# Moving the merge-gate jobs of a two-branch decoder block into nine dense head chunks, with a merged rotation and a shorter softmax

## The reference, cut to what matters

```python
def hybrid_mixer(h, w_in, ..., w_proj_a, w_proj_b, w_out, layer_idx):
    z = jnp.einsum('bsd,dn->bsn', h, w_in)
    qa, ka, va, ga, qb, kb, vb, gb, fl, ma, mb = jnp.split(z, idx, axis=-1)
    # 8 differential heads: partial rotation of q and k, two softmax maps, a = p0 - lam * p1
    oa = rmsnorm(diff_attention(rope(qa), rope(ka), va, lam), g_subln) * (1.0 - lam_init)
    ya = (oa * silu(ga)) @ w_proj_a
    # 8 forgetting ("fox") heads: one softmax map, bias from the summed log forget gates
    yb = (forgetting_attention(qb, kb, vb, log_f) * silu(gb)) @ w_proj_b
    m = jax.nn.sigmoid(ma) * ya + jax.nn.sigmoid(mb) * yb
    return jnp.einsum('bsd,de->bse', m, w_out)

def reference(x, ...):
    x = x + hybrid_mixer(rmsnorm(x, g_norm), ...)
    return rmsnorm(x, g_final)
```

## Time and profile before

| | us |
|---|---|
| median of 3 runs | 741.78 (741.42 to 742.18) |
| the profiled execution | 742.65 |
| its span, first to last instruction | 740.8 |
| TensorE busy | 729.5 (98%) |
| VectorE busy | 566.1 (76%) |
| ScalarE busy | 437.8 (59%) |
| GpSimd busy | 126.3 (17%) |

### The profile page before, as it was taken

How to read it: one execution, slowest core, us unless ns; L and a number is a source line. 1 busy time by engine, 2 the same in 40 slices (tenths; PEclk the granted TensorE clock), 3 DMA queues, 4 the chain that set the end, 5 groups by cost and what they waited for, 6 DMA issues and landing times.

```text
span 740.8 us, 9801 instructions
## 1 busy us (share of the span) xinstructions
PE 729.5 (98%) x3538; PEld 609.9 (82%) x3538; DVE 566.1 (76%) x746; ACT 437.8 (59%) x654; POOL 126.3 (17%) x153
## 2 busy tenths in 40 slices
PE   9999999999999999999999999999999999999996
PEld 6998888888888888888878888788888888888885
DVE  6775798788779878868979976979998757655552
ACT  7963767566656565665656766667567444444531
POOL 0000223103010203030615030704050000001110
PEclk9999999999999999999999999999999999999999
DMA  8668365776947686775576876666777756755632
GB/s 330 213 214 328 139 227 209 248 225 239 343 158 252 214 263 211 275 289 185 220 243 198 269 252 252 223 233 215 215 257 230 220 185 227 297 188 190 192 140 114
DMA packets 47230, 168.97 MB, mean 228 GB/s; under 512 B 5256, under 2 KB 5264, under 8 KB 46672
## 3 DMA queue, kind: packets, MB, share of 16 engines
q1 hardware_dynamic: 46064, 164.97, 65.1%
q10 hardware_dynamic: 864, 1.84, 0.7%
q0 software_dynamic: 256, 1.54, 0.5%
HBM read 166.23 MB, written 2.11 MB: 227 GB/s over the span
## 4 chain that ended last, share of the span: by engine, by line
PE 90%; POOL 4%; DVE 2%; issue 2%; DMA 1%; ACT 1%; SPq 0%; DVEq 0%; POOLq 0%; ACTq 0%
PE Z L338 27%; PE Z L340 27%; PE Z L339 27%; PE Z L499 3%; POOL rope_t L1223 3%; PE A L440 1%; DVE w_lo L841 1%; PE A L406 1%; DMA w_raw<-in_w_main 1%; PE B L422 1%; PE B L419 1%; POOL z_sb L1228 1%; PE Dk L431 1%; DVE gates L908 1%; POOL z_sb L1229 1%
## 5 line engine op out<-in xcount | busy, mean ns | idle before, releaser
L841 DVE TENSOR_TENSOR w_lo<-w_raw,w_hi 128x1024 fp32r<-128x1024 f32 (+1 forms) x240 | 290.4, 1215 | 111.3 <-ACT w_hi L610 108.7
L610 ACT ACTIVATE w_hi<-w_raw 128x1024 fp32r<-128x1024 f32 (+1 forms) x235 | 243.6, 1044 | 187.0 <-PE Z L340 164.5
L338 PE MATMUL Z<-w_hi,hT_hi 128*128 128x512 f32 (+2 forms) x720 | 274.6, 381 | 0.5 <-DVE w_lo L841 0.5
L340 PE MATMUL Z<-w_hi,hT_lo 128*128 128x512 f32 (+2 forms) x720 | 272.8, 379 | 0.0
L339 PE MATMUL Z<-w_lo,hT_hi 128*128 128x512 f32 (+2 forms) x720 | 272.6, 379 | 0.0
L338 PEld LDWEIGHTS Z<-w_hi,hT_hi 128*128 128x128 f32 x720 | 135.3, 188 | 26.6 <-issue 0.6
L340 PEld LDWEIGHTS Z<-w_hi,hT_lo 128*128 128x128 f32 x720 | 135.3, 188 | 25.7
L339 PEld LDWEIGHTS Z<-w_lo,hT_hi 128*128 128x128 f32 x720 | 135.4, 188 | 24.6
L338 PE MATMUL Z<-w_hi,sum_hi 128*128 128x512 f32 x256 | 101.2, 395 | 0.0
L340 PE MATMUL Z<-w_hi,sum_lo 128*128 128x512 f32 x256 | 99.9, 390 | 0.0
L339 PE MATMUL Z<-w_lo,sum_hi 128*128 128x512 f32 x256 | 99.7, 389 | 0.0
(11 more groups left out here) (184 smaller groups left out, 593.7 us busy)
## 6 DMA issues: line engine op xcount, KB each, us to landing
w_raw<-in_w_main SPq DMA_DIRECT2D x283, 512.0 KB, 4.2
x_and_g<-in_w_main SPq DMA_DIRECT2D x16, 512.0 KB, 6.3
w_raw<-in_w_fl SPq DMA_DIRECT2D x8, 264.0 KB, 3.1
o_T<-in_x SPq DMA_DIRECT2D x1, 2048.0 KB, 8.0
x_and_g<-in_xT SPq DMA_DIRECT2D x4, 256.0 KB, 5.9
gates<-c_rows_dram POOLq DMA_DIRECT2D x1, 1024.0 KB, 5.7
z_sb<-in_g_final SPq DMA_DIRECT2D x1, 1024.0 KB, 10.0
x_and_g<-in_xT ACTq DMA_DIRECT2D x3, 256.0 KB, 7.2
```

The costliest lines, as they stand in the source:

```text
L338: pe.matmul(acc, a_hi, b_hi, start=first, stop=False)
L340: return pe.matmul(acc, a_lo, b_hi, start=False, stop=last)
L610: act.activation(w_hi[:, t % RING, 0:cols_of(t)], weights(t), ACT.Copy).then_inc(hi_ready, 1)
L841: dve.tensor_tensor(w_lo[:, t % RING, 0:n], weights(t), w_hi[:, t % RING, 0:n].bitcast(fp32), ALU.subtract).then_inc(lo_ready, 1)
```

## The change

Chunks 3 to 11 carry twelve merge jobs each, chunk 12 carries four, and chunks 2, 13, 14, 15 and the fox projections carry none (`SUMS_IN`, `ORDER`). The number of jobs, their weights and their matmuls stay the same, and so does each group's order of forms. A chunk without merge jobs, and each projection, takes the other pair of PSUM banks than the one before it (`PAIR`), and `banks_free` waits for the last user of that pair. The places of the bursts X and Y are set for each kind of chunk. The rotation works on both token halves at once: four products and two sums of 128 x 64. The masked maximum gives the negative scaled value at once, so that the small multiplication behind it is gone. The two maps are combined in one pass, with the first normalizer carried to the output's scaling, where one small product is added. The last quarter row is squared on VectorE instead of ScalarE.

```diff
 FL_JOB, VG_JOB, PLAIN_JOB, MIXED_JOB = 8, 16, 20, 28
-FOX_JOB = MIXED_JOB + 16 * (N_HEADS - 3)
-FOX2_JOB = FOX_JOB + 16
-DIFF_JOB = FOX2_JOB + 8
+SUMS_IN = {3: 12, 4: 12, 5: 12, 6: 12, 7: 12, 8: 12, 9: 12, 10: 12, 11: 12, 2: 0, 12: 4, 13: 0, 14: 0, 15: 0}
+ORDER = {0: 'hhhhhhhh', 4: 'hshshshshhhh', 12: 'hshsshshsshshsshhsss'}
+CHUNK_JOB = [0, 0, PLAIN_JOB]
+for c in range(3, N_HEADS + 1):
+    CHUNK_JOB.append(CHUNK_JOB[-1] + len(ORDER[SUMS_IN[c - 1]]))
+FOX_JOB = CHUNK_JOB[N_HEADS]
+DIFF_JOB = FOX_JOB + 16
 OUT_JOB = DIFF_JOB + 16
 JOBS = OUT_JOB + 32
-HEAD_STEPS, SUM_STEPS = (0, 2, 4, 6, 8, 10, 12, 13), (1, 3, 5, 7, 9, 11, 14, 15)
-FOX_STEPS, FOX_SUM_STEPS = (0, 2, 4, 5, 8, 11, 14, 15), (1, 3, 6, 7, 9, 10, 12, 13)
-SUM_JOB = ([MIXED_JOB + 16 * c + u for c in range(N_HEADS - 3) for u in SUM_STEPS] + [FOX_JOB + u for u in FOX_SUM_STEPS])
+SUM_JOB = [CHUNK_JOB[c] + u for c in range(2, N_HEADS) for u, kind in enumerate(ORDER[SUMS_IN[c]]) if kind == "s"]
 SUM_OF = {job: s for s, job in enumerate(SUM_JOB)}
-X_AT = {21: 0, 28: 1, 38: 2, **{MIXED_JOB + 16 * (b - 2) + 4: b for b in range(3, N_HEADS)},
-        FOX2_JOB + 1: N_HEADS, DIFF_JOB + 1: N_HEADS + 1}
-Y_AT = {25: 0, 33: 1, 43: 2, **{MIXED_JOB + 16 * (b - 2) + 9: b for b in range(3, N_HEADS)}, FOX2_JOB + 5: N_HEADS}
+BURST_X, BURST_Y = {0: 2, 4: 4, 12: 5}, {0: 6, 4: 9, 12: 11}
+X_AT = {21: 0, 28: 1, 40: 2, **{CHUNK_JOB[b + 1] + BURST_X[SUMS_IN[b + 1]]: b for b in range(3, N_HEADS - 1)},
+        FOX_JOB + 2: N_HEADS - 1, FOX_JOB + 9: N_HEADS, DIFF_JOB + 1: N_HEADS + 1}
+Y_AT = {25: 0, 34: 1, 46: 2, **{CHUNK_JOB[b + 1] + BURST_Y[SUMS_IN[b + 1]]: b for b in range(3, N_HEADS - 1)},
+        FOX_JOB + 5: N_HEADS - 1, FOX_JOB + 13: N_HEADS}
 C_ZERO, C_MASK, C_TRI, C_IDENT, C_ONE = 0, P, 2 * P, 3 * P, 4 * P
...
+def max_count(heads):
+    return 2 * heads + 2 * max(0, heads - HEADS)
+
+
 def head_job(c, j):
     if c == 0:
         return j
-    return PLAIN_JOB + j if c == 2 else MIXED_JOB + 16 * (c - 3) + HEAD_STEPS[j]
+    return CHUNK_JOB[c] + [u for u, kind in enumerate(ORDER[SUMS_IN[c]]) if kind == "h"][j]
 def fox_job(n, j):
-    return FOX_JOB + FOX_STEPS[4 * n + j] if n < 2 else FOX2_JOB + 4 * (n - 2) + j
+    return FOX_JOB + 4 * n + j
...
 PARTS_AT = {PLAIN_JOB + 7: 0, MIXED_JOB + 2: 1, MIXED_JOB + 11: 2, MIXED_JOB + 18: 3}
-O_SPLIT_AT = {FOX_JOB - 20: 0, FOX_JOB - 14: 1, FOX2_JOB + 3: 2, FOX2_JOB + 4: 3}
+O_SPLIT_AT = {CHUNK_JOB[13] + 4: 0, CHUNK_JOB[13] + 7: 1, CHUNK_JOB[15] + 4: 2, FOX_JOB + 7: 3}
 HEAD_OF = {head_job(c, j): (c, j) for c in range(2, N_HEADS) for j in range(TILES)}
 FOX_OF = {fox_job(n, j): (n, j) for n in range(4) for j in range(4)}
 DIFF_OF = {diff_job(n, j): (n, j) for n in range(4) for j in range(4)}
+
+
+PAIR = [0, 1, 0, 1]
+for c in range(3, N_HEADS):
+    PAIR.append(0 if SUMS_IN[c] else 1 - PAIR[-1])
+for n in range(11):
+    PAIR.append(1 - PAIR[-1])
+LAST_PAIR = 1 - PAIR[-1]
+FIRST_SUM_FILL, FOX_FILL, DIFF_FILL, OUT_FILL = 4, 17, 21, 25
...
                 mm.then_inc(w_used, 1)
-            def banks_free(fill):
-
-                pe.wait_ge(evac[0], fill - 1)
-                pe.wait_ge(evac[1], fill - 1)
+            def banks_free(fill, pair):
+
+                before = [n for n in range(fill) if PAIR[n] == pair]
+                if before:
+                    pe.wait_ge(evac[0], before[-1] + 1)
+                    pe.wait_ge(evac[1], before[-1] + 1)
+                if pair == 1 and fill > FIRST_SUM_FILL:
+                    form_taken(FORMS * GROUPS - 2)
+                    form_taken(FORMS * GROUPS - 1)
             def z_tile(c, j):
-                tile(head_job(c, j), 1 if c == 2 else 0, hT_hi, hT_lo, 2 * j, 2, CHUNK, j == 0, j == TILES - 1)
+                tile(head_job(c, j), PAIR[fill_of(c)], hT_hi, hT_lo, 2 * j, 2, CHUNK, j == 0, j == TILES - 1)
...
                     if j == 0:
-                        banks_free(4 if c == 3 else fill_of(c) + 1)
+                        banks_free(fill_of(c), PAIR[fill_of(c)])
                     z_tile(c, j)
...
                 if j == 0:
-                    banks_free((18, 19, 19, 20)[n])
-                    if n == 2:
-                        form_taken(FORMS * GROUPS - 2)
-                        form_taken(FORMS * GROUPS - 1)
+                    banks_free(FOX_FILL + n, PAIR[FOX_FILL + n])
                 if n == 0:
                     pe.wait_ge(o_split, j // 2 + 1)
-                tile(fox_job(n, j), 1 if n == 2 else 0, oT_hi, oT_lo, 2 * j, 2, CHUNK, j == 0, j == 3)
+                tile(fox_job(n, j), PAIR[FOX_FILL + n], oT_hi, oT_lo, 2 * j, 2, CHUNK, j == 0, j == 3)
             for job in range(FOX_JOB, DIFF_JOB):
-                if job in FOX_OF:
-                    fox_tile(*FOX_OF[job])
-                else:
-                    sum_tile(SUM_OF[job])
+                fox_tile(*FOX_OF[job])
                 attention(job)
...
             def exps(h):
-                act.wait_ge(max_ready, h + 1)
-                maps, scale = (1, HD ** -0.5) if h < HEADS else (2, QK ** -0.5)
+                act.wait_ge(max_ready, max_count(h + 1))
+                maps, scale = 1 if h < HEADS else 2, -1.0
                 for i in range(maps):
...
                 for m in range(M_TILES):
-                    ins = act.activation(og[:, m, :], A[:, m * P:(m + 1) * P], ACT.Square,
+                    ins = act.activation(og[:, m, :], A[:, m * P:(m + 1) * P], ACT.Square, scale=inv[:, m:m + 1],
                                          accum_out=o_ssq[:, m:m + 1])
...
                     S = (B, C)[i]
-                    counted(dve.tensor_tensor_reduce(probs[:, i, 0:P], S[:, 0:P], add0, 1.0, NEG, ALU.add, ALU.max,
-                                                     row_max[:, 2 * i:2 * i + 1]))
-                    n = counted(dve.tensor_tensor_reduce(probs[:, i, P:3 * P], S[:, P:3 * P], add1, 1.0, NEG, ALU.add, ALU.max,
-                                                         row_max[:, 2 * i + 1:2 * i + 2]))
-                dve.wait_ge(dve_step, n)
-                if h < HEADS:
-                    ins = dve.tensor_scalar(neg_max[:, 0:2], row_max[:, 0:2], -(HD ** -0.5), None, ALU.mult)
-                else:
-                    ins = dve.tensor_scalar(neg_max[:], row_max[:], -(QK ** -0.5), None, ALU.mult)
-                ins.then_inc(max_ready, 1)
+                    scale = -(HD ** -0.5) if h < HEADS else -(QK ** -0.5)
+                    dve.tensor_tensor_reduce(probs[:, i, 0:P], S[:, 0:P], add0, scale, -NEG, ALU.add, ALU.min,
+                                             neg_max[:, 2 * i:2 * i + 1]).then_inc(max_ready, 1)
+                    dve.tensor_tensor_reduce(probs[:, i, P:3 * P], S[:, P:3 * P], add1, scale, -NEG, ALU.add, ALU.min,
+                                             neg_max[:, 2 * i + 1:2 * i + 2]).then_inc(max_ready, 1)
             def head_qkT_lo(h):
...
                     chained(dve.reciprocal(inv[:], sums[:]))
-                    chained(dve.tensor_scalar(inv[:, 2:4], inv[:, 2:4], neg_lam[:, 0:1], None, ALU.mult))
+                    chained(dve.scalar_tensor_tensor(inv[:, 2:4], inv[:, 2:4], neg_lam[:, 0:1], sums[:, 0:2], ALU.mult, ALU.mult))
             def combine_maps(h):
                 for m, sl in enumerate((slice(0, P), slice(P, 3 * P))):
-                    n = counted(dve.tensor_scalar(probs[:, 1, sl], probs[:, 1, sl], inv[:, 2 + m:3 + m], None, ALU.mult))
-                dve.wait_ge(dve_step, n)
-                for m, sl in enumerate((slice(0, P), slice(P, 3 * P))):
-                    ins = dve.scalar_tensor_tensor(probs[:, 0, sl], probs[:, 0, sl], inv[:, m:m + 1],
-                                                   probs[:, 1, sl], ALU.mult, ALU.add)
+                    ins = dve.scalar_tensor_tensor(probs[:, 0, sl], probs[:, 1, sl], inv[:, 2 + m:3 + m],
+                                                   probs[:, 0, sl], ALU.mult, ALU.add)
                 ins.then_inc(probs_ready, 1)
...
                     dve.wait_ge(o_rstd_ready, h - HEADS + 1)
-                    factor = o_rstd
+                    chained(dve.tensor_tensor(o_factor[:], o_rstd[:], inv[:, 0:2], ALU.mult))
+                    factor = o_factor
                 dve.wait_ge(dve_step, gate_step)
...
                                   ALU.add).then_inc(evac[m], 1)
-                dve.wait_ge(y_squared, 7 + part)
+                if part == 2:
+                    dve.wait_ge(evac[1], 30)
+                    n = counted(dve.tensor_tensor_reduce(m_b[:, 0, 0:CHUNK // 2], y_sb[:, m, cols], y_sb[:, m, cols], 1.0 / D_MODEL,
+                                                         0.0, ALU.mult, ALU.add, y_ssq[:, 1, 4:5]))
+                    dve.wait_ge(dve_step, n)
+                else:
+                    dve.wait_ge(y_squared, 7 + part)
                 dve.wait_ge(y_ms_ready, 2 + part)
...
                     pool.wait_ge(rope_ready, h - HEADS)
-                for m in range(M_TILES):
```

(31 more changed lines are left out.)

25 lines of the change are left out of this document (12 added, 13 removed).

## The result

The changed kernel takes 757.6 us (median of 5 runs, 756.62 to 758.46), the kernel before 742.18 (5 runs on the same chip, 741.42 to 744.12): a ratio of 1.021, 95% interval 1.0198 to 1.0223. Slower, as forecast, but by 15.4 us where I had said 3.7, and outside the range.

A forecast was written before the change was run, and what follows sets the result against it. The prediction took TensorE's matmul stream as the bound. From the profiled 742.65 us, - 2.4 (rotation) + 3.1 (VectorE) + 3.0 (loads) = 746.35; with the median 0.87 below the profiled execution, 745.5 us, range 739.4 to 751.0.

The forecast's parts named there:

- The matmul stream as the bound: TensorE, busy 729.5 of 740.8 us, sets the time; the change can only win where it stands still mid-kernel.
- what the arithmetic gives: TensorE's waits for GpSimd's rotation, 2.4 us together, go: the most the new order and merged rotation can give back.
- the rival of a late rotation: In the short chunks the larger rotation operations make TensorE wait, 7.5 us at four heads; median 746.9, chance 0.05.
- The VectorE term: Dense chunks: TensorE waits 3.1 us for VectorE's splits; 4.7 if priced higher, 1.9 if the count is too strict.
- The count: Lead plus TensorE's time less VectorE's work falls short at five dense places: -1.8 (jobs 203 to 206), -0.6 (186), -0.7 (113).
- the cap: With four ring slots, the splits' lead can't exceed the three jobs between less 2.5 us.
- the step on the bank pairs: Chunks 4 to 12: reusing a bank pair waits 1.5 us for ScalarE's evacuation, covered by s s s (4.1 us); priced nothing.
- The loads term: Nine dense chunks: late loads cost 0.33 us per chunk, 3.0 us, with bounds of 0 and 7.5 us.
- The absorbing lead: In dense chunks the splits' lead absorbs the density and only the rotation's waits go; median 739.4, chance 0.20.
- VectorE late alone: In dense chunks VectorE is late as counted, the loads never are; median 742.5, chance 0.15.
- The loads at their upper bound: Loads are late at every dense chunk, 7.5 us, each delayed split delaying the load behind it; median 750.0, chance 0.17.
- What I named to look for: Chunks 3 to 11: 3 to 10 us of weight waits, longest near 2 in chunk 11; VectorE over 90% busy.

The follow-up runs named there:

- kernel 1: Kernel before, old job order, given only the change's merged rotation, shorter softmax and last square on VectorE: 740.08 us, ratio 0.9972.
- kernel 4: Changed kernel with the middle jobs' loads bringing half of each block (256 KB), the rest stale and the result wrong: 747.19 us, ratio 1.0068.
- kernel 9: Changed kernel with a fifth raw slot, its room coming from shared buffers: 746.68 us, ratio 1.0062.
- kernel 12: Changed kernel with half loads (wrong result), and ScalarE's evacuation of a finished head chunk after the next rounding instead of before: 744.62 us, ratio 1.0032.
- Kernel 10: Changed kernel with a fifth raw slot, and ScalarE's evacuation at a chunk's end after the next rounding instead of before: 745.68 us, ratio 1.0048.
- Kernel 3: Changed kernel with VectorE's 64 adds working on 32 of 1024 columns, loads, waits and order kept, merge gates wrong: 740.29 us, ratio 0.9975.
- kernel 8: Changed kernel with eleven chunks of ten merge jobs and one of two, instead of nine of twelve and one of four: 749.18 us, ratio 1.0093.

## Why the prediction was right in sign and wrong in size

**The matmul stream as the bound, and what the arithmetic gives: right.** The rotation's waits went, no other came; -2.4 counted, -1.9 measured (kernel 1, with an interval of about 1 us to each side). The short chunks lost nothing, so the rival of a late rotation is out: beside VectorE an operation of 128x64 costs what one of 128x32 did. The tail gained 0.07, inside the 0 to 0.1 taken as nothing. `banks_free` shows no wait; the banks cost one of 0.3 us, at the first merge job (`PE Z L355 <- ACT z_sb L631`).

**The VectorE term: mis-sized, 3.1 for about 7.** With loads out of the way 7.1 us (kernel 4) or 6.6 (kernel 9) remain, above my upper bound of 4.7; by starts of matmuls their stalls sum to 6.2 and 4.9. The count failed in the cap. I wrote that the lead after job t can't exceed three jobs less 2.5 us for rounding, split and hand-overs; where a head chunk ends, ScalarE has the evacuation to do before that rounding, so it is less 3.8. Putting the evacuation behind the split is worth 2.6 us with the loads early (kernel 12), and the stalls at three chunks' first jobs go with it. (Kernel 10, with five slots, shows only 1.0, with stalls of its own in chunk 3.) I did count this evacuation, but only in the step on the bank pairs, as something that s s s covers for TensorE, and did not ask who stands behind it in ScalarE's own queue. With it 3.1 would be near 5.7. What is left of the difference, about 1 us, I can't assign to a row. Nor was the count right place by place. Of the three with a number, 113 is there in kernel 4 as counted (0.65 for 0.7), 206 is much smaller (0.73 for 1.8), and 186 isn't there (188 is a chunk's first job, behind an evacuation). There are small ones that the count did not have: 58, 65, 66, 68, 153, 158, 188 and 208.

**The loads term: mis-sized, 3.0 for about 10.5, and its upper bound of 7.5 was no bound.** I priced a late load at the 0.83 us by which ScalarE had waited before, once per dense chunk. Two things are wrong in this. Loads of this kernel take 4.2 us in the median, but the ones ahead of job 111 took 7.1 and 7.9 (issued 247.50 and 247.87, landed 254.56 and 255.80), and four slots turning in 6.8 us leave no room for that. The kernel before had as many slow loads, 20 over 6 us; what it had besides is lead. And the load is waited for not by ScalarE alone but by VectorE at an add, at the head of a queue that is 86% busy in the stretch (354.4 of 411.35): what it stands there it has no slack to make up, and the raw slots that it would have freed come later. A stand of 1.61 us became a stall of 2.35: from the end of job 110's split (251.77) to the end of job 111's VectorE needs 3.6 us for two folds, an add and a split, besides its stand, while TensorE's head job between lasts 2.7. The lead that could have paid for that was gone, after a stand of 0.72 us at the add before. Kernels 4 and 9 take away the loads' lateness in two unrelated ways, half the bytes and one more slot, and give back 10.4 and 10.9.

**The sum of the two as a sum: wrong in form.** Kernel 3 shows it: with the adds short, the loads are as large and as long in flight as before (median 4.2 us) and only 0.2 us are lost. I had one chain (load, add, rounding, split, slot free, load) and cut it into two independent prices.

**Rivals.** The absorbing lead (739.4) is out: it needed a shortfall of VectorE under 0.5 us at each place. VectorE late alone (742.5) is out, as loads cost the most. The loads at their upper bound (750.0) had the right mechanism, a delayed split that delays its load, and too small a price. What I named to look for came in part: the waits for `w_hi` and `w_lo`, 13.2 us in the list, the longest 2.2, ScalarE's waits for loads at 24.0 us, no GpSimd. I had taken `ACT w_hi` as the sign of a late load; it is no sign of it, since all these waits end with a split. Wrong was VectorE's share of over 90% in dense chunks as a sign of the loss: it was 92% in chunk 6, which lost nothing, and 76% in chunk 7. The longest stalls were at jobs 58 and 111 (2.4 us each); the one in chunk 11, at job 206, was 1.9.

**What stays open.** Why density matters already at ten merge jobs (kernel 8: 1.0093 - 0.9972 = 0.0121 of the kernel before, 9.0 us over kernel 1, where I expected 1 to 4; some 6 are stalls by starts and 1.6 the clock behind one of them), why the late evacuation brings new stalls in chunk 3 with full loads, and which of the small places of VectorE's remainder belong to hand-overs. A version of kernel 1's arithmetic with a fifth slot was not run; with 0.24 us of stalls left in kernel 1's middle there is little for it to gain.
